# Two blocks of a transformer on one core: the order and width of the matmuls of a mixed tile

## The reference, cut to what matters

```python
bcx = h @ w_in                        # 1024 x 3072
...
return (jax.nn.silu(g) * u) @ w_down  # 2816 x 1024, twice
...
proj = jnp.einsum("bsd,dc->bsc", u, w_in)          # 1024 x 7168
y_attn = attn @ w_branch_attn
y_lru = (hl * jax.nn.gelu(g_lru)) @ w_branch_lru
merged = jax.nn.sigmoid(gate_attn) * y_attn + jax.nn.sigmoid(gate_lru) * y_lru
...
m = jnp.square(jax.nn.relu(u @ w_mlp_up[l])) @ w_mlp_down[l]
```

## Time and profile before

| | us |
|---|---|
| median of 3 runs | 985.37 |
| lowest, highest | 985.01, 987.43 |
| the profiled execution, its own time | 978.75 |
| its span in the profile | 977.0 |
| PE busy in it | 970.0 |
| DVE, ACT, POOL busy | 696.9, 589.4, 268.0 |

### The profile page before, as it was taken

How to read it: one execution, slowest core, us unless ns; L and a number is a source line. 1 busy time by engine, 2 the same in 40 slices (tenths; PEclk the granted TensorE clock), 3 DMA queues, 4 the chain that set the end, 5 groups by cost and what they waited for, 6 DMA issues and landing times.

```text
span 977.0 us, 19940 instructions
## 1 busy us (share of the span) xinstructions
PE 970.0 (99%) x7076; PEld 902.9 (92%) x7076; DVE 696.9 (71%) x1046; ACT 589.4 (60%) x1050; POOL 268.0 (27%) x241
## 2 busy tenths in 40 slices
PE   9999999999999999999999999999999999999998
PEld 7999899999998899999999888888889989998887
DVE  7987766665668778666565799987877877664443
ACT  7556755554557767545554678968585577664332
POOL 2431233220102223223210136542031546441000
PEclk9999999999999999999999999999999999999999
DMA  9785565655543245555455554654444536556531
GB/s 335 256 316 187 188 212 174 213 167 190 206 173 129 88 138 207 198 189 204 164 203 205 176 177 165 216 181 164 173 147 170 201 130 218 205 179 207 181 130 43
DMA packets 37712, 180.92 MB, mean 185 GB/s; under 512 B 3472, under 2 KB 7824, under 8 KB 19984
## 3 DMA queue, kind: packets, MB, share of 16 engines
q1 hardware_dynamic: 37504, 179.99, 52.5%
q10 hardware_dynamic: 144, 0.08, 0.1%
HBM read 179.01 MB, written 1.05 MB: 184 GB/s over the span
## 4 chain that ended last, share of the span: by engine, by line
PE 95%; DVE 2%; ACT 1%; issue 1%; POOL 1%; DMA 1%; SPq 0%; POOLq 0%; DVEq 0%
PE bank L502 26%; PE bank L496 19%; PE bank L498 17%; PE bank L500 17%; PE bank L540 4%; PE bank L539 4%; PE bank L538 4%; DVE wlo L1534 1%; DVE xa L1588 1%; PE bank L751 1%; PE bank L626 1%; DMA x<-in_x 1%; PE bank L735 1%; PE bank L765 0%; PE bank L976 0%
## 5 line engine op out<-in xcount | busy, mean ns | idle before, releaser
L1534 DVE TENSOR_TENSOR wlo<-raw,whi 128x1024 fp32r<-128x1024 f32 (+1 forms) x289 | 354.2, 1226 | 148.0 <-ACT whi L1009 147.1
L1009 ACT ACTIVATE whi<-raw 128x1024 fp32r<-128x1024 f32 (+2 forms) x289 | 302.1, 1046 | 202.2 <-PE bank L502 196.7
L502 PE MATMUL bank<-xa,wlo 128*128 128x256 f32 x1536 | 308.7, 277 | 0.0
L502 PEld LDWEIGHTS bank<-xa,wlo 128*128 128x128 f32 x1536 | 254.9, 188 | 22.9
L498 PE MATMUL bank<-xa,whi 128*128 128x256 f32 x904 | 227.3, 276 | 0.0
L500 PE MATMUL bank<-xa,whi 128*128 128x256 f32 x904 | 227.2, 276 | 0.0
L496 PE MATMUL bank<-xa,whi 128*128 128x512 f32 x632 | 203.3, 397 | 0.7 <-POOL wlo L2242 0.5
L498 PEld LDWEIGHTS bank<-xa,whi 128*128 128x128 f32 x904 | 169.7, 188 | 0.0
L500 PEld LDWEIGHTS bank<-xa,whi 128*128 128x128 f32 x904 | 169.7, 188 | 0.0
L2130 POOL TENSOR_TENSOR gate<-act,rbc 128x256 f32<-128x256 f32 x44 | 69.0, 1569 | 158.2 <-ACT act L1174 153.0
L496 PEld LDWEIGHTS bank<-xa,whi 128*128 128x128 f32 x632 | 99.6, 188 | 7.6 <-issue 1.7
(11 more groups left out here) (233 smaller groups left out, 1530.0 us busy)
## 6 DMA issues: line engine op xcount, KB each, us to landing
raw<-in_stream SPq DMA_DIRECT2D x137, 1024.0 KB, 4.8
raw<-in_stream SPq DMA_DIRECT2D x42, 512.0 KB, 4.8
raw<-in_stream SPq DMA_DIRECT2D x8, 768.0 KB, 4.1
bias<-in_bias SPq DMA_DIRECT2D x1, 3072.0 KB, 11.4
raw<-in_stream SPq DMA_DIRECT2D x8, 256.0 KB, 5.5
x<-in_x SPq DMA_DIRECT2D x4, 256.0 KB, 5.4
out<-x SPq DMA_DIRECT2D x3, 256.0 KB, 2.2
cons<-in_cons SPq DMA_DIRECT2D x1, 576.0 KB, 9.1
```

The lines of the kernel that those rows point to most:

```text
L502: ins = pe.matmul(narrow, wlo[:, slot, at + i, :], X[:, k, 0, :], start=False, stop=last and i == len(tiles) - 1)
L1009: act.activation(whi[:, p, 0:kts, :].rearrange("p k m -> p (k m)"), src, ACT.Copy)\
L1534: dve.tensor_tensor(wlo[:, p, 0:kts, :].rearrange("p k m -> p (k m)"), src, whi[:, p, 0:kts, :].rearrange("p k m -> p (k m)").bitcast(F32) ...
```

## The change

`blocks` gets a branch: a mixed tile whose eight k-tiles come in one call goes to the new `whole_tile`. That issues hi for the k-tiles 0 to 2, then the lo of the k-tiles 0 and 1 (where the slot is odd) or 0 to 3 (where it is even), then hi for the k-tiles 3 to 5, then the other lo up to the k-tile 5. For k-tiles 6 and 7 the matmul of 512 columns is replaced by two of 256, one into each half of the bank, and followed by the lo. A tile had 16 matmuls, 8 of 512 columns and 8 of 256; it has 18, 6 of 512 and 12 of 256. The columns in all are the same, 6144. The products and where they are summed are unchanged, as are all instructions of the other engines, the waits ahead of a tile and the count after it. All other calls of `blocks` go on as before.

```diff
+            def whole_tile(slot, X, dst):
+
+                narrow, apart = dst[:, 0:TOK], dst[:, TOK:2 * TOK]
+                between = 2 if slot % 2 else 4
+
+                def lo(k):
+                    return pe.matmul(narrow, wlo[:, slot, k, :], X[:, k, 0, :], start=False, stop=k == KT - 1)
+                for k in range(6):
+                    pe.matmul(dst, whi[:, slot, k, :], X[:, k, :, :], start=k == 0, stop=False)
+                    if k == 2:
+                        for i in range(between):
+                            lo(i)
+                for k in range(between, 6):
+                    lo(k)
+                for k in range(6, KT):
+                    pe.matmul(narrow, whi[:, slot, k, :], X[:, k, 0, :], start=False, stop=False)
+                    pe.matmul(apart, whi[:, slot, k, :], X[:, k, 1, :], start=False, stop=False)
+                    ins = lo(k)
+                return ins
+
             def blocks(slot, X, tiles, dst, first, last, at=0):
 
+                if dst.shape[1] == 2 * TOK and len(tiles) == KT:
+                    return whole_tile(slot, X, dst)
                 narrow = dst[:, 0:TOK]
```

## The result

| | us |
|---|---|
| before, median of 14 executions (range) | 985.56 (979.34 to 988.39) |
| with the change, median of 14 (range) | 978.64 (978.12 to 979.33) |
| ratio, 95% interval | 0.9936 (0.9921 to 0.9952) |
| profiled execution before: own time, span | 978.75, 977.0 |
| profiled execution after: own time, span | 978.66, 976.9 |

The change makes the kernel faster by 0.64%, 6.9 us, where 1.65 us were forecast and 981.3 us was the lower end of the range. And yet the two traces span the same to 0.1 us. The two facts have one cause, and the table already shows it: before, executions lie 9 us apart, after, 1.2 us, and the one execution of before that was traced was faster than all 14 that were timed. The granted clock is full (0.999 or 1.0) in both traces and in all 14 executions of the change.

A forecast was written before the change was run, and what follows sets the result against it. PE was taken to bound the kernel, busy 970.0 of 977.0 us. 66 mixed tiles saving 25 ns each give 1.65 us, so 985.37 - 1.65 = 983.7 us; range 981.3 to 987.0 us.

The forecast's parts named there:

- What bounds: Whole kernel: PE, busy 970.0 of 977.0 us at full clock, bounds; time is the sum of its steps.
- The narrow end of the tile: Last two k-tiles of a mixed tile: 0 to 11 ns saved per tile, half-bank writes taken as free.
- The threes: Mixed tiles: three hi end the surcharge cycle, leaving lo clean; 2736 ns a tile against 2761, 25 ns less.
- if they are clean, two or four between make no difference: Mixed tiles: whether two or four lo stand between the threes makes no difference, if clean; no cost given.
- 24 steps and 2720 ns a tile: Narrow tiles: 113.3 ns a step of 256 columns, 24 steps, 2720 ns a tile.
- The difference carries over.: Whole kernel: the median before is 6.6 us above the profiled execution, and this stays: 985.37 - 1.65 = 983.7 us.
- The 24 tiles behind float32: Tiles of `g2`, `ga`, `gl` among attention's matmuls: start out of step, some 20 ns dearer, same gain of 25 ns.
- The covers: Weights' rounding has three tiles, over 8 us; PE's later waits are 0.5 us or less; nothing becomes late.
- B: Mixed tiles: order gives nothing, 2760 ns a tile, no change, 985.4 us; chance 0.12.
- C: Mixed tiles: lo stay slow behind threes, +35 to +77 ns a tile, 987.7 to 990.5 us; chance 0.12.
- A: All 66 mixed tiles: every surcharge goes, 2720 ns a tile, 3.1 us saved, 982.3 us; chance 0.12.
- a chance of the starting moment: Mixed tiles: the whole basis would be wrong if the cycle of three is this, not a grouping rule; no size.

The follow-up runs named there:

- one form throughout: The change with the same number of lo between the threes in every slot: four, 993.75 us; two, 985.05 us.
- fours: The 66 mixed tiles as four hi, four lo, four hi, four lo, in place of the change's order: 995.24 us.
- six well placed tiles: New form only for the last mixed tile ahead of each of six narrow stretches, other 60 in pairs as in the kernel before: 978.72 us.

## Why the prediction was wrong

**What bounds: right.** PE bounds, the granted clock is full, no wait of others matters. The pricing from start to start was also right, and found the thing itself: steps of 113 or 118 for the same matmul, depending on what went before.

**The narrow end of the tile: right.** The half-bank writes are free; the four added matmuls of a clean tile run at 276.

**The threes: right in mechanism and size for a clean tile.** 2736 was forecast and 2734 measured. As a term of the sum, 66 x 25 ns = 1.65 us, they were mis-sized all the same: between two traces without a slow stretch the spans differ by 0.1 us, as the two paragraphs on the 24 tiles and on the covers show. But "if they are clean, two or four between make no difference" passed over the case in which they are not. The runs with one form throughout cost 6 and 15 us there, in the stretches behind.

**The step that failed: "24 steps and 2720 ns a tile" as a fixed price of a narrow tile.** I read 113.3 ns from one trace and took it as a property of narrow tiles. It is one of two rhythms, and the other, 117.8, was in the same rows, as the slow lo behind an incomplete three. I had asked what the surcharge does to the next lo and the next hi, and never what it does to a run of 256-column matmuls that has no hi to end the cycle. It keeps it. 3944 narrow matmuls (twice 1394 and twice 578) in the four stretches behind mixed tiles of `bx`, `up0`, `up1` and `mup`, 4.45 ns each, were outside the sum (with `bl` 4138 in all).

**"The difference carries over."** 6.6 us lay between the profiled execution and the median, and three timed runs were 2.4 us apart. I added the 6.6 us as a constant. It was the effect: the traced execution had all five long stretches in the good rhythm, and by their times 13 of the 14 timed ones had not. The range took in only a 1 us spread for it, so it ended at 981.3 us, above the lowest group of the kernel before itself. An upper bound for what the change could gain, in any trace, is not to be had from a trace of the best execution.

**The 24 tiles behind float32: wrong sign.** I left them the same gain of 25 ns. Timeline of the change, answering:

```profile
644.86 1.05 PE L497 MATMUL bank<-xb,whi 128*128 128x512 f32 x3
...
647.85 0.49 PE L891 MATMUL bank<-cons,pr 128*128 128x128 f32 x3
648.10 0.95 PE L497 MATMUL bank<-xb,whi 128*128 128x512 f32 x3
...
650.96 0.38 PE L906 MATMUL bank<-pt,vtok 128*128 128x128 f32 x2
```

Less the drain (1.05 and 0.95 where a clean three prints 0.85) they take 2.79 and 2.76 us; before it was 2.78 twice. Over all 24 the step sums give 8 ns more a tile than before: +0.2 us, not -0.6. Single tiles lie between 49 ns less and 40 ns more. A tile that starts out of step has more matmuls of 256 columns to pay with; that this is the reason is an argument and not shown.

**The covers: one failed, a little.** Among the tiles of `x2` to `k2` PE now arrives early and waits for `wlo`. The last tile begins 2.83 us after the one before it, when this DVE instruction ends at 603.66:

```profile
601.89 1.77 DVE L1556 TENSOR_TENSOR wlo<-raw,whi 128x1024 fp32r<-128x1024 f32 x1
...
603.72 0.50 PE L497 MATMUL bank<-xa,whi 128*128 128x512 f32 x1
```

That is 0.1 us, and as much again one tile on. So between the two traces, both in the good rhythm, the 42 plain tiles gained 0.8 us without these two losses (1.1 forecast), and the rest gave nearly all of it back: the 24 tiles 0.2, these waits 0.2, and 0.2 in the first 20 us, where no tile of the change has run yet. 0.1 us is left.

**The rivals.** B, that the order gives nothing, and C, that the lo stay slow, are both refuted for the change; C is what fours and the single forms do. A, every surcharge gone, came nearest in size, 3.1 us of 6.9, and its mechanism did not happen: hi still prints 388, 392 and 394. The last sentence of the prediction came near the danger, a chance of the starting moment, and I gave it no price.

## What to carry to other kernels

A median far above the profiled execution, or timed runs some tenths of a per cent apart on a kernel without waits, are a finding to be explained before anything is predicted: trace the kernel again until a dear execution is caught, and count matmuls in fixed windows. Compare the change with the lowest group of executions as well as with the median. Price a regrouping of matmuls also by the rhythm in which it leaves the stretch behind it; six well placed tiles were worth as much as 66. When a form brings PE back in step, test it from more than one starting point.

## What the runs showed of the hardware that I had not expected

- A run of back-to-back 256-column float32r matmuls, each with its own load of weights, goes at 113.3 or at 117.8 ns a step, at the same granted clock (1.00), and keeps the step for 1394 matmuls, through the turns of a loop. What comes right before it decides, and a matmul that starts some 0.1 us late can change it, either way.
- The same 512-column matmul takes 225 to 237 ns from start to start where nothing is late. After a clean start three in a row cost 226, 230 and 232 and leave the next matmul clean; two or four leave it slow.
- The Trainium skill (TensorE: Matmul & The Clock Gate, "Wait — 56ns, not 53.3ns?") gives columns by 2.4 GHz and some 2.5 ns, by which a step would be 109 and 216 ns. No stretch of these matmuls here reached that (113.3 and 226 ns at best), and that section has one step for a size at full clock where the traces have several.
- What inside PE keeps the two rhythms apart is open. The runs show which sequences enter and leave them, not what is being waited for.
